# Mixer layer of a two-layer decoder trunk: new order of the first loads and of the input products

## The reference, cut to what matters

```python
p = rmsnorm(h, e_norm_mix) @ e_w_in            # 1024 -> 512 (pool) + 512 (u) + 512 (v)
a_in = p[..., :512]
z = gelu(p[..., 512:])                         # u and v
y_a = pool_mixer(a_in, e_pool_w, e_pool_scale) # trailing means over 2, 4, 8, 16, minus the token, then a 128x128 map per group
y_b = spatial_gating(z, ln_g, ln_b, ws, bias)  # u * (tril(W_s) @ layernorm(v) + b), per 128 tokens and head
h = h + concat([y_a, y_b]) @ e_w_out           # 1024 -> 1024
hn = rmsnorm(h, e_norm_ffn)
h = h + (silu(hn @ wg) * (hn @ wu)) @ wd       # width 2816
```

## Time and profile before

| | us |
|---|---|
| median of 3 runs | 1636.23 |
| lowest and highest run | 1636.18, 1641.57 |
| the profiled execution's own time | 1636.89 |
| its span (first to last instruction) | 1635.1 |
| PE, PEld busy | 1559.2, 1301.7 |
| DVE, ACT busy | 1232.4, 964.8 |
| DMA | 424.17 MB, mean 259 GB/s |

### The profile page before, as it was taken

How to read it: one execution, slowest core, us unless ns; L and a number is a source line. 1 busy time by engine, 2 the same in 40 slices (tenths; PEclk the granted TensorE clock), 3 DMA queues, 4 the chain that set the end, 5 groups by cost and what they waited for, 6 DMA issues and landing times.

```text
span 1635.1 us, 21896 instructions
## 1 busy us (share of the span) xinstructions
PE 1559.2 (95%) x8074; PEld 1301.7 (80%) x8074; DVE 1232.4 (75%) x1475; ACT 964.8 (59%) x1105; POOL 6.0 (0%) x9
## 2 busy tenths in 40 slices
PE   6789999699999997999999999999999999999996
PEld 5449999568879956888888888888888888888885
DVE  2335545540677427999999999999999999999997
ACT  2124444240142215887887887887887887887884
POOL 0000000000000000000000000000000000000000
PEclk9889999799999998999999999999999999999999
DMA  9436653402000447998999998998998999999960
GB/s 348 156 119 205 211 173 112 155 0 103 24 1 30 140 158 284 379 371 325 377 371 326 376 372 324 376 373 324 375 374 324 375 374 325 372 374 330 368 248 26
DMA packets 192886, 424.17 MB, mean 259 GB/s; under 512 B 6929, under 2 KB 31649, under 8 KB 192706
## 3 DMA queue, kind: packets, MB, share of 16 engines
q1 hardware_dynamic: 191058, 421.08, 71.0%
q10 hardware_dynamic: 1488, 1.31, 0.3%
q0 software_dynamic: 288, 1.05, 0.2%
HBM read 422.38 MB, written 1.05 MB: 259 GB/s over the span
## 4 chain that ended last, share of the span: by engine, by line
PE 94%; DVE 3%; DMA 1%; ACT 1%; issue 1%; SPq 0%; DVEq 0%; POOL 0%
PE psum L1371 19%; PE psum L1373 19%; PE psum L1372 19%; PE psum L531 7%; PE psum L1963 4%; PE psum L1964 4%; PE psum L1965 4%; PE psum L1352 2%; PE psum L1919 2%; PE psum L357 2%; PE psum L805 2%; PE psum L1389 1%; PE psum L608 1%; PE psum L691 1%; PE psum L701 1%; PE psum L1926 1%
## 5 line engine op out<-in xcount | busy, mean ns | idle before, releaser
L1531 DVE TENSOR_TENSOR w_lo<-ring,w_hi 128x1024 fp32r<-128x1024 f32 x672 | 804.7, 1224 | 43.9 <-ACT w_hi L1462 3.9
L1462 ACT ACTIVATE w_hi<-ring 128x1024 fp32r<-128x1024 f32 x672 | 712.7, 1064 | 179.8 <-PE psum L1373 179.7
L1371 PE MATMUL psum<-w_hi,xg_split 128*128 128x512 f32 x896 | 354.3, 395 | 3.6 <-DVE xg_split L1623 3.6
L1373 PE MATMUL psum<-w_lo,xg_split 128*128 128x512 f32 x896 | 350.1, 391 | 0.0
L1372 PE MATMUL psum<-w_hi,xg_split 128*128 128x512 f32 x896 | 349.4, 390 | 0.0
L1371 PEld LDWEIGHTS psum<-w_hi,xg_split 128*128 128x128 f32 x896 | 168.7, 188 | 37.5 <-DVE xg_split L1623 3.8
L1373 PEld LDWEIGHTS psum<-w_lo,xg_split 128*128 128x128 f32 x896 | 168.5, 188 | 35.9
L1372 PEld LDWEIGHTS psum<-w_hi,xg_split 128*128 128x128 f32 x896 | 168.9, 188 | 33.7
L1371 PE MATMUL psum<-w_hi,ht_split 128*128 128x512 f32 x448 | 175.1, 391 | 0.0
L1373 PE MATMUL psum<-w_lo,ht_split 128*128 128x512 f32 x448 | 174.4, 389 | 0.0
L1372 PE MATMUL psum<-w_hi,ht_split 128*128 128x512 f32 x448 | 174.3, 389 | 0.0
(11 more groups left out here) (299 smaller groups left out, 1608.5 us busy)
## 6 DMA issues: line engine op xcount, KB each, us to landing
ring<-o_moe_wg_dram SPq DMA_DIRECT2D x56, 2048.0 KB, 7.9
ring<-o_moe_wu_dram SPq DMA_DIRECT2D x56, 2048.0 KB, 8.1
ring<-o_moe_wd_dram SPq DMA_DIRECT2D x56, 2048.0 KB, 7.8
ring<-e_ffn_wg_dram SPq DMA_DIRECT2D x11, 1024.0 KB, 5.5
ring<-e_ffn_wu_dram SPq DMA_DIRECT2D x11, 1024.0 KB, 9.3
ring<-e_ffn_wd_dram SPq DMA_DIRECT2D x11, 1024.0 KB, 11.2
ring<-e_w_in_dram SPq DMA_DIRECT2D x3, 2048.0 KB, 18.1
ring<-e_w_out_dram SPq DMA_DIRECT2D x2, 2048.0 KB, 20.2
```

The source lines that it names most:

```text
L1371: nc.tensor.matmul(dst, x_hi, hi, start=first, stop=False)
L1373: return nc.tensor.matmul(dst, x_hi, lo, start=False, stop=last_)
L1462: nc.scalar.activation(w_hi[:, (4 * i + n) % 4, :], piece(i, n), ACT.Copy).then_inc(m_hi, 1)
L1531: V.tensor_tensor(w_lo[:, r, :], piece(i, n), w_hi[:, r, :].bitcast(F32), ALU.subtract).then_inc(m_lo, 1)
```

## The change

The host packs the gain vectors into one array of 128x144 (`columns`). SP loads x in two blocks, then the v part of the input weights in two halves of the contraction, the pool part, the constants without the identity, the u part, and the output weights. ACT's queue loads the identity and the packed columns first; the five loads of 256 KB come after ACT's part of norm 0's copies, the gate's matrices first. ACT runs one root on a constant ahead of x.

PE transposes and begins the v product at once, piece by piece of `xnT` as the copies finish, for both blocks in turn. The gate matrices' transposes follow, then the four pool groups, u group 0, the gate's products, u groups 1 and 2, the pool maps, u group 3, and the output product, whose first group waits for each gate head singly. DVE does the LayerNorm and the mask first, then the pool path, then bias and product with u head by head. PSUM banks are changed to fit. In ACT's and DVE's streams the first four weight pieces of the SwiGLU are split before norm 1. PE no longer waits for all four adds and for all of the split rows, but for each pair of them inside its first SwiGLU group. The arithmetic is the same; SwiGLU chunk 0 is now loaded after the v and the pool products (six counts), chunk 1 after ten, as before.

```diff
@@ SP
-            sp.dma_start(h[:, :, :], I["x"].rearrange("b (n p) d -> p (b n) d", p=P)).then_inc(s_x, 16)
-            sp.dma_start(cst[:, :], cst_dram[:, 0:CW]).then_inc(s_cst, 16)
...
-                    sp.dma_start(colsrc[at:at + n, base * P:base * P + P], flat).then_inc(s_colsrc, 16)
...
+            for b in range(TB):
+                sp.dma_start(h[:, b, :], I["x"][0, b * P:(b + 1) * P, :]).then_inc(s_x[b], 16)
...
-            for k in range(3):
-                sp.dma_start(w8(k), win[:, :, 512 * k:512 * k + 512]).then_inc(slot_in[k], 16)
+            sp.dma_start(w8(0)[:, 0:4, :], win[:, 0:4, 1024:1536]).then_inc(s_vhalf, 16)
+            sp.dma_start(w8(0)[:, 4:KT, :], win[:, 4:KT, 1024:1536]).then_inc(slot_in[0], 16)
+            sp.dma_start(w8(1), win[:, :, 0:512]).then_inc(slot_in[1], 16)
+            sp.dma_start(cst[:, P:CW], cst_dram[:, P:CW]).then_inc(s_cst, 16)
+            sp.dma_start(w8(2), win[:, :, 512:1024]).then_inc(slot_in[2], 16)
@@ ACT
+            act.dma_start(cst[:, 0:P], cst_dram[:, 0:P]).then_inc(s_id, 16)
+            act.dma_start(cols[:, :], cols_dram).then_inc(s_cols, 16)
+            act.wait_ge(s_one, 1)
+            nc.scalar.activation(small[:, 501:502], small[:, 500:501], ACT.Sqrt)
+            norm_act(act, 0)
+            act.wait_ge(s_cols, 16)
+            norm_cols(0, "e_norm_mix")[0](act)
...
+            for g in range(3):
+                u_gelu(g)
...
+            u_gelu(3)
...
+            def piece_hi(i):
+                what, c, n = FPIECES[i]
+                act.wait_ge(ffn_in[c % 4], 48 * (c // 4 + 1))
+                if i >= 4:
+                    act.wait_ge(f_pc, i - 3)
+                nc.scalar.activation(as_piece(f_hi, i, what), ffn_piece(what, c, n), ACT.Copy).then_inc(f_phi, 1)
+
+            for i in range(4):
+                piece_hi(i)
             norm_act(act, 1)
@@ DVE
+            for g in range(4):
+                dve.wait_ge(g_ev, 4 + g)
+                nc.vector.tensor_tensor(mixT[:, 4 + g, :], mixT[:, 4 + g, :], uT[:, g, :], ALU.mult).then_inc(s_mix, 1)
+            if reached(2):
+                dve.wait_ge(s_mix, 4)
+                for i in range(4):
+                    f_piece_lo(i)
             add_to_h(dve, s_wo, (1, 2, 3, 4), 1)
@@ PE
+            pe.wait_ge(s_id, 16)
             norm_pe(pe, 0)
-            norm_ready(pe, 0)
...
+            for n, k in enumerate((0, 2, 1, 3, 4, 6, 5, 7)):
+                if n == 0:
+                    pe.wait_ge(s_vhalf, 16)
+                if n == 4:
+                    pe.wait_ge(slot_in[0], 16)
+                pe.wait_ge((n_eva, n_evd)[n % 2], n // 2 + 1)
+                for b in range(TB):
+                    last = nc.tensor.matmul(psum[:, b, :], xnT[:, k, b * P:(b + 1) * P], w8(0)[:, k, :],
+                                            start=(n == 0), stop=(n == KT - 1))
+                    if n == KT - 1:
+                        last.then_inc(p_in, 1)
+            pe.wait_ge(s_small, 80)
+            for g in range(4):
+                last = nc.tensor.transpose(psum[:, 2, g * P:(g + 1) * P], r3(E_["ws"], 4)[:, g, :], ident)
+            last.then_inc(s_wsT, 1)
...
+            pe.wait_ge(slot_in[1], 16)
+            for g in range(4):
+                turned_product(w8(1), g, 4 + g)
+            pe.wait_ge(slot_in[2], 16)
+            turned_product(w8(2), 0, U_BANK[0])
+            pe.wait_ge(s_vn, 2)
+            pe.wait_ge(s_wsTm, 1)
+            for q in range(2):
+                pe.wait_ge(a_ev, 3 + q)
+                gate_mixed(q)
+            pe.wait_ge(g_ev, 2)
+            turned_product(w8(2), 1, U_BANK[1])
+            turned_product(w8(2), 2, U_BANK[2])
+            pe.wait_ge(s_pooled, 1)
...
+            turned_product(w8(2), 3, U_BANK[3])
...
-            pe.wait_ge(s_h, 4)
             norm_pe(pe, 1)
-            norm_ready(pe, 1)
...
+                            if (c, w, j, k % 2) == (0, 0, 0, 0):
+                                pe.wait_ge(n_evd, 4 + k // 2 + 1)
```

More of the change, by code:

```diff
@@ L97, with columns, trunk @@
         _base += _n
-def trunk(nc, I, cst_dram, out, stop=None, probe=None):
+def columns(inputs):
+    order = [name for group in (COLUMNS, COLUMNS2) for name, _ in group]
+    return np.ascontiguousarray(np.concatenate([np.asarray(inputs[name]).reshape(-1, P) for name in order]).T)
+def trunk(nc, I, cst_dram, cols_dram, out, stop=None, probe=None):
     ctx = ExitStack()
@@ L1724, in _ @@
                 if c == 0:
[L1725 removed]
+                    sp.wait_ge(p_in, 6)
                 if c == 1:
@@ L1812, in _ @@
         def _(dve):
+            nc.vector.memset(small[:, 500:501], 1.0).then_inc(s_one, 1)
             a, s, t = (r3(E_[x], 4) for x in "ast")
@@ L1930, in _ @@
-            pe.wait_ge(g_ev, 4)
-            for g in range(4):
-                last = nc.tensor.transpose(psum[:, 6, g * P:(g + 1) * P], r3(E_["ws"], 4)[:, g, :], ident)
-            last.then_inc(s_wsT, 1)
-            pe.wait_ge(s_pooled, 1)
-            pe.wait_ge(a_ev, 4)
-            for g in range(4):
-                nc.tensor.matmul(psum[:, 2 + g, 0:T], r3(E_["pw"], 4)[:, g, :], pooled[:, g, :],
-                                 start=True, stop=True).then_inc(s_ymm, 1)
-            pe.wait_ge(s_vn, 2)
@@ L1940, in _, with gate_mixed @@
-            pe.wait_ge(s_wsTm, 1)
-            for q in range(2):
+            def gate_mixed(q):
                 for g in (2 * q, 2 * q + 1):
@@ L1948, in _ @@
                 last.then_inc(s_mm, 1)
-            pe.wait_ge(slot_in[3], 16)
-            pe.wait_ge(slot_in[4], 16)
-            pe.wait_ge(s_mix, 2)
-            pe.wait_ge(s_yev, 4)
-            pe.wait_ge(g_ev, 6)
-            rows_product(pe, mixT, lambda q: w8(3 + q), 0, s_wo)
+            pe.wait_ge(slot_in[1], 16)
+            for g in range(4):
+                turned_product(w8(1), g, 4 + g)
[10 more added lines that the diff above has]
+            pe.wait_ge(s_pooled, 1)
+            for g in range(4):
+                last = nc.tensor.matmul(psum[:, 4 + g // 2, (g % 2) * T:(g % 2 + 1) * T], r3(E_["pw"], 4)[:, g, :],
+                                        pooled[:, g, :], start=True, stop=True)
+                if g % 2 == 1:
+                    last.then_inc(s_ymm, 1)
+            turned_product(w8(2), 3, U_BANK[3])
+            pe.wait_ge(s_yev, 4)
+            for n in range(4):
+                pe.wait_ge(slot_in[3 + n % 2], 16)
+                if n == 2:
+                    pe.wait_ge(g_ev, 7)
+                for k in range(KT):
+                    if n == 0 and k >= 4:
+                        pe.wait_ge(s_mix, k - 3)
+                    last = nc.tensor.matmul(psum[:, n, :], mixT[:, k, (n // 2) * P:(n // 2 + 1) * P], w8(3 + n % 2)[:, k, :],
+                                            start=(k == 0), stop=(k == KT - 1))
+                last.then_inc(s_wo, 1)
             if not reached(2):
                 return
-            pe.wait_ge(s_h, 4)
             norm_pe(pe, 1)
-            norm_ready(pe, 1)
             def three(dst, l_hi, l_lo, r_hi, r_lo, first, last_):
```

127 lines of the change are left out of this document (52 added, 75 removed).

## The result

The changed kernel took 1616.83 us (median of 4 runs, 1615.23 to 1617.56) against 1636.3 for the kernel before; the ratio is 0.9874, 95% interval 0.9858 to 0.9890. The profiled execution took 1617.56 us with a span of 1615.7. The forecast was 1615 and the sign and the size held. Several terms of the sum did not: the start, with the first product group, gave 3.6 us more than predicted and the hole around the LayerNorm 5.6 less, and the two stood against each other.

A forecast was written before the change was run, and what follows sets the result against it. The mixer was taken as PE work with three holes: the start, the LayerNorm of v and norm 1. Savings of 7.4 + 10.6 + 3.5 = 21.5 us gave 1615 us, with an 8-in-10 range of 1609 to 1621.5.

The forecast's parts named there:

- Start: Before the first product: fewer bytes ahead let v start at 12.9 us instead of 20.3, saving 7.4 us.
- x's landing: At the start: x block 0 with identity and columns lands at 6.5 us, bounds 5.4 and 8.5.
- The cold first group: First product group: the 1.85 us lost to the cold clock stays in full, now inside v; no gain.
- The moved loads: Behind the v product: PE waits for all five loads, landed at 29.3 to 29.5, adding 1.0 us; bounds 0 and 4.4.
- the correction of the flight: Fifth moved load: 3.6 us taken off its 17.1 us flight because 5 us had flowed at 102 instead of 356 GB/s.
- The rival of 0.17: Moved loads land at 32.9, 3.4 us more, and TensorE cools, another 2.5; time 1621, chance 0.17.
- The first hole: PE's idle stretch around the LayerNorm of v: 16.2 us shrink to 5.6 with the new wait, saving 10.6.
- The cover of the LayerNorm: LayerNorm and mask end at 40.4 behind other products; PE asks at 47.2, 7 us later.
- Norm 1: Output product to first SwiGLU product: PE starts after one split pair, 5.7 us instead of 9.27, saving 3.5.
- The sum: Whole kernel: 7.4 + 10.6 + 3.5 = 21.5 us saved, for a time of 1615.
- Slower: ACT's and DVE's streams stop for SwiGLU chunk 0 before norm 1; slower if it lands past 106.5; chance 0.01.

The follow-up runs named there:

- e10: Changed kernel with the five 256 KB loads issued right behind the columns, ahead of ACT's part of norm 0, still one semaphore; 1609.75 us, ratio 0.9841.
- e8: e7 plus twelve filler transposes on PE ahead of those of norm 0; 1605.38 us, ratio 0.9811.
- e1: Changed kernel with the five moved loads on four semaphores, one for each consumer, each waited for where used; 1608.08 us, ratio 0.9821.
- e2: Changed kernel with the load of the constants behind the u weights instead of ahead of them; 1615.39 us, ratio 0.9856.
- e3: Changed kernel, but PE waits for all eight copies of the turned rows before the v product; 1614.48 us, ratio 0.9854.
- e4: Changed kernel with the part around norm 1 undone: full waits for adds and split rows, first weight pieces split after norm 1; 1619.32 us, ratio 0.9883.
- e6: e1 with PE waiting for the whole LayerNorm of v right behind the gate transposes; 1622.07 us, ratio 0.9907.
- e7: e1 with seven filler products on PE where it waits in norm 1; 1608.86 us, ratio 0.9848.
- e5: Kernel before with the new start alone (new loads, packed columns, root on a constant), old order of products; 1627.01 us, ratio 0.9937.
- e9: Repeat of e5, the kernel before with the new start alone; 1628.27 us, ratio 0.9958.
- e11: e1 with twelve filler transposes ahead of norm 0's, without fillers in norm 1; 1608.66 us, ratio 0.9813.
- e12: Repeat of e8, e1 with both fillers, run beside e11; 1607.95 us, ratio 0.9824.

## Why the prediction was right, and where it was not

- **Start (7.4 predicted, 9.1 measured).** The step that failed is x's landing: 5.09 us instead of 6.5, and even under the lower bound of 5.4. The bound took the 102 GB/s of the first 5 us for a property of the start. The changed kernel moved 181 GB/s there, and byte counting held for the rest: v's weights were not waited for. What had made the start slow can't be parted fully. The DMA engines of the kernel before, first 5 us (q10 is ACT's queue, q1 SP's):

```profile
DMA packets 185, 0.51 MB, mean 102 GB/s; under 512 B 6, under 2 KB 6, under 8 KB 185
...
q10 hardware_dynamic: 115, 0.22, 30.5%
q1 hardware_dynamic: 70, 0.29, 29.3%
```

  Only 6 pieces were under 2 KB, and the rows of the 14 small loads have 512 bytes, so these loads are hardly the cause. The five loads on ACT's queue had moved 115 pieces of some 2 KB. SP's queue had moved 70 pieces of 4 KB, and a piece of these held an engine for 0.33 us (29.3% of 16 engines' 5 us, over 70), against 0.16 us a piece, of 3.8 KB on average, in the changed kernel (41.7%, 204 pieces). That points to the five loads ahead of x, which e10 doesn't rebuild: there they stood behind the identity and the columns and had moved next to nothing by 5 us. x in one load and the constants right behind it are left as rivals; no run parts them.
- **The cold first group (0 predicted, 1.85 gained).** I kept it, since transposes had not cured it before. In the changed kernel v ran from its first product at the full rate (13.90 us), and in e8 transposes alone brought the clock up. Over the runs that begin with v and have no fillers, v took 13.97, 14.69, 13.97, 14.88, 14.83, 14.11 and 14.00 us (e1, e2, e3, e4, e6, e7, e10), so the loss there is 0 to 1 us. The three profiled executions that begin with the pool product lost more, 1.85 us before and 2.6 and 2.5 in e5 and e9, behind the same sixteen transposes. Idling between transposes and products doesn't explain it: it was 1.0 us in e9 and 1.2 in e3, and e3's v was not slow. So this gain came with the new order of the products and not with the start; why, no run tells. The prediction cited the page "TensorE: Matmul & The Clock Gate" of the Trainium skill, Part 4, that transposes do not count as activity in the same way, and said that the trace agreed. The runs do not agree: e8, e11 and e12 show sixteen transposes in 2.64, 2.62 and 3.25 us behind twelve fillers, where every run without fillers took 3.46 to 3.67.
- **The moved loads (1.0 predicted, 7.3 measured).** Their landing came out as forecast, 29.42 against 29.3 to 29.5, but by two errors that cancelled. The fifth load was issued at 13.03 and not at 15.8 (13.4 + 2.4), and it flew 16.4 us and not 13.5. The step that failed here is the correction of the flight: the row of 17.1 us, taken as it is, was 0.7 off, in this kernel and in e2 (16.4), e3 (16.3) and e4 (16.7), and the 3.6 us that I took off it had no ground. What turned 1.0 us of wait into 4.4 is the other side: v ended at 25.09 instead of 28.5, by the faster start and the warm first group. So 3.4 of the 3.6 us that the start and the first group gave beyond the forecast went into this wait, and with it a cold stretch of 2.9 that the sum didn't have. The rival of 0.17 had this wait (4.4) and this cold stretch (2.5), but with loads landing at 32.9, which they didn't. That this surplus and this loss nearly cancel is luck in part, and in part no accident, since a load that lands at a fixed time swallows whatever the work ahead of it gains.
- **The first hole (10.6 predicted, 5.0 measured).** Gate transposes 1.11 and not 0.45, since cold; gate 1.78 against 2.4; pool maps 1.73 against 1.75; wait 4.4; 2.2 us in the first pool group. 16.2 - 11.2 = 5.0 in place of 10.6. The cover of the LayerNorm held: the last of it ended at 35.4, PE asked at 50.1, and e6 prices the cover at 12.0.
- **Norm 1 (3.5 predicted, 3.6 measured).** 5.70 us from the output product's end, as predicted to the digit; the SwiGLU's half clock lasted 6.1 instead of 5.8 us. e4 confirms the term.
- **The sum.** 9.1 + 1.85 + 5.0 + 3.6 = 19.6, against 21.5. The medians differ by 19.5.
- **Slower.** SwiGLU chunk 0 never decided: ACT's first split ran at 64.28, right behind u's gelu, and no add waited for it.

What stays open: why the clock falls in one wait of 3 us and not in another (e3 and e2 had 2.9 and 3.6 us of idling), why a pool product in front begins colder than v does, and whether the fillers are worth their 0.9 and 1.3 us of the traces in the time too.

## What to carry to other kernels

A semaphore that several loads share is as late as the last of them: when the loads are moved, look at who waits for the full count, and give each consumer its own. Price a wait on TensorE with the cold stretch behind it; here 4.4 us of waiting cost 7.3. A wait is the difference of two times: where the load's landing is fixed, each microsecond gained ahead of it goes into the wait. Take a load's flight from a row of the same traffic as it is; the correction made here was wrong by 2.9 us. And look at who issues the loads: five issues on ACT ahead of the norm (e10) cost 1.1 us though no byte was late.

## What the runs showed of the hardware

- Transposes raise TensorE's clock: with twelve fillers ahead, sixteen transposes took 2.64 and 2.62 us, in a third run 3.25, instead of 3.46 to 3.67, with nothing but transposes before them.
- The clock after a short wait is not fixed by the kernel. e5 and e9 are one kernel and waited 1.7 us ahead of the output product; its first 3 us were granted at 0.50 in e5 and at 1.00 in e9, and the product took 30.7 and 27.8 us. Ahead of the gate transposes the clock was half until 5.5 us into the next products after 4.4 us of waiting (changed kernel), stayed full after 2.9 us in e3, and fell after 3.6 us in e2 and e4.
- The first 5 us moved 102 GB/s with the five loads of 256 KB in front, x in one load and the constants behind it, and 181 GB/s with the identity and the columns in front and x in two loads. At most 6 pieces of the 14 small loads had moved by then.
- Issuing five loads kept ACT busy from 1.63 to 4.77 us in e10, and its table load came only then.
- Putting the 1.2 MB load of long rows behind another brought four loads, one of 512-byte rows and three of 2 KB rows, some 2 us sooner (10.4 to 8.3 us, 13.1 to 11.2); the fifth landed after 16.4 us in both.
